# The look-up of expert numbers in a routed layer, split into a short and a long half

## The chip, the cores and the metric

The kernel runs on one core of a Trainium2 chip. The metric is the device time of one execution in microseconds (us). The core has a tensor engine (PE), a vector engine (DVE), a scalar engine (ACT), GpSimd (POOL) and a queue engine (SP), which run on their own and wait for one another by semaphores, and 16 DMA engines.

## The reference

One layer over 1024 tokens of 1024 fp32 numbers: a mixing sublayer (window attention beside a gated delta rule), and a sublayer that routes each token to single experts. The routing is what matters here:

```python
q = jnp.einsum('bsd,de->bse', h, w_query).reshape(B, S, PEER_HEADS, 2, PEER_QUERY_DIM // 2)
scores = jnp.einsum('bshpd,hpnd->bshpn', q, sub_keys)
s_top, i_top = lax.top_k(scores, K)                                   # K = 16, 8 heads, 2 x 128 keys
cand = (s_top[..., 0, :, None] + s_top[..., 1, None, :]).reshape(B, S, PEER_HEADS, K * K)
best, ci = lax.top_k(cand, K)
expert = i1 * N_KEYS + i2              # i1, i2: the keys of candidate ci
gates = jax.nn.softmax(best, axis=-1)
...
u = jnp.take(expert_u, et, axis=0)     # 128 experts for each token
act = jax.nn.gelu(jnp.einsum('tkd,td->tk', u, xt), approximate=False) * gt
return jnp.einsum('tk,tkd->td', act, jnp.take(expert_v, et, axis=0))
```

So each token reads 128 rows of `expert_u` and 128 of `expert_v`, of 4 KB each: 1.07 GB for the whole sequence.

## The kernel before, in words

The tokens are cut into 8 tiles of 128. A tile's work on the way to its experts is written as pieces numbered 0 to 49, and each engine has its own part of a piece. Pieces 0 to 22 are the mixing and the layer norm after it, 23 to 30 the products with the query weights (PE alone), 31 to 36 the search for the 16 best keys of each of the 16 key sets, and 37 to 49 the rest of the routing on DVE:

- Piece 37 forms the candidates. The 16 best of 256 sums can only be among 50 pairs (i, j), those with (i+1)(j+1) at most 16. `PAIR_ROWS` lists them by blocks, and for each block one addition writes the sums (`cand`) and one the expert numbers (`cid`), over all 8 heads: 14 additions at L2001.
- Pieces 38 and 39 find the 16 best candidates of each head in order, as values (`best`) and as places 0 to 49 (`fbest`).
- Pieces 40 to 47 look up the expert numbers, a head each. L2035 compares 16 ranks x 50 places, L2039 multiplies the hits with the numbers, and L2042 sums each rank's 50. Each of the three waits for the one before it.
- After piece 47 PE turns the numbers (piece 48, L1273). DVE copies them in pieces 48 (L2050) and 49 (L2066) into what POOL reads, and releases POOL by `g_tile`. POOL then gathers: 128 rows of U (one slot for 128 tokens, L944) and 128 of V (one token's 128 experts, L952, or L964 and L969 where V rows also go into U's buffers), each an indirect DMA of 512 KB.

DVE multiplies each U row with the tokens (the dot products, L2074), and PE sums V rows with the gates as weights (L1326). U and V have 8 buffers each. POOL waits at L943 until DVE or PE has freed a U buffer.

The order of pieces is written out by hand in tables of "halves": after each two dot products (or four in tile 0) every engine does the pieces that its table puts at this half. Tile 0 has nothing beside its pieces but input projections (units of 8 matmuls at L301, done by PE beside pieces 0 to 22 and 31 to 41, in its order ahead of piece 48). Tile 1's pieces go beside and after tile 0's dot products by `VECTOR_AT`: pieces 37 to 49 stand at halves 70 to 83, past the last dot product, mixed with pieces 1 to 4 of tile 2 (`EARLY_MIX`). Among those, piece 2 writes the coefficients that PE waits for at L1154, and piece 4 waits for PE at L1722. Tile 2's routing pieces stand at halves 33 to 61 of tile 1's dot products (`FIRST_TAIL`), between the mixing of tile 3. From then on a loop does the same for each tile (`TAIL` and `MIX`).

The lists of a tile (`top`, `itop`, `ftop`, `cand`, `cid` and so on) are views of one stretch of 2048 numbers in each partition, `arena` for tile 0 and the last eighth of `wq` for the others; `eq`, the 800 hits, lies over `top`, `itop` and `ftop`, which are read out by then. `gl` holds the gelu of the dot products, `actT` its transpose, from which ACT fills the columns of weights (`fill`).

Of the kernel before, what the change touches and what calls it, by code (L numbers as in the profile page):

```python
# [18 lines left out]
P = 128  # L19
# [8 lines left out]
PH, NK, TOPK = 8, 128, 16  # L28
SLOTS = PH * TOPK
# [6 lines left out]

PAIR_ROWS = [(0, 1, 16, 0), (1, 2, 8, 16), (2, 3, 5, 24), (3, 4, 4, 29), (4, 5, 3, 33), (5, 8, 2, 36), (8, 16, 1, 42)]
NCAND = 50
LEAST = -3.0e38
NU = 8  # L40
NV = 8
# [71 lines left out]
CONST_COLS = {}  # L113
_at = 0
for _name, _n in (("ident", P), ("upto", P), ("after", P), ("decay_mask", P), ("ones", 1), ("chunk_of", 2),
                  ("level", 6 * P), ("ident_a", P), ("dist", 192), ("dist_past", 64), ("iota50", 50)):
    CONST_COLS[_name] = (_at, _at + _n)
    _at += _n
NCONST = _at
# [16 lines left out]
def constant_table():  # L136

    t = np.zeros((P, NCONST), np.float32)

    def put(name, a):  # L140
        lo, hi = CONST_COLS[name]
        t[:, lo:hi] = a.reshape(a.shape[0], -1)
# [10 lines left out]
    for l in range(6):  # L153
        b = 1 << l
        j, i = r[:, None], r[None, :]
# [7 lines left out]
    dist = np.where(ok, np.abs(q - k), FAR).astype(np.float32)  # L163
    put("dist_past", dist[:, 0:64])
    dist[:, 0:64] = FAR
    put("dist", dist)
    put("iota50", np.tile(np.arange(50, dtype=np.float32)[None], (P, 1)))
    return t


def build(nc, consts, x, ln_in_g, ln_in_b, w_in, conv_w, a_sinks, b_a_log, b_dt_bias, b_norm_w, w_out,
          ln1_g, ln1_b, w_query, sub_keys, expert_u, expert_v, ln2_g, ln2_b, out):
    fp32, u32 = mybir.dt.float32, mybir.dt.uint32
    ALU, ACT, AX = mybir.AluOpType, mybir.ActivationFunctionType, mybir.AxisListType

    ctx = ExitStack()
    with ctx:
        def sb(name, shape, dt=fp32, c=ctx):
            return c.enter_context(nc.sbuf_tensor(name, shape, dt))
# [7 lines left out]
        s_dve = sem("s_dve")  # L187
# [5 lines left out]
        def const(name):  # L193
            lo, hi = CONST_COLS[name]
            return C[:, lo:hi]
# [477 lines left out]
        h1T = view(0, KD, P)  # L673
        qT = view(1024, 2 * PH, P)
        w_part = view(1024, 2 * PH * P)
        Lists = namedtuple("Lists", "top itop ftop cand cid best ibest fbest fex den eq")

        def lists(at):

            return Lists(at(0, 2 * PH, TOPK), at(256, 2 * PH, TOPK, dt=u32), at(512, PH, 2, TOPK),  # L680
                         at(800, PH, NCAND), at(1200, PH, NCAND), at(1600, PH, TOPK), at(1728, PH, TOPK, dt=u32),
                         at(1856, PH, TOPK), at(800, PH, TOPK), at(1984, 2, PH), at(0, TOPK, NCAND))

        def last_view(at, *dims, dt=fp32):
            return shaped(wq[:, KD - 1, at:at + int(np.prod(dims))], dims, dt)
# [3 lines left out]
        def lists_for(t):  # L689

            return lists_of[0 if isinstance(t, int) and t == 0 else 1]
# [27 lines left out]
        eidx = sb("eidx", [P, 2, SLOTS], u32, c=b)  # L719
        eidxT = sb("eidxT", [P, 2, P], u32, c=b)  # L720
        dots = sb("dots", [P, SLOTS], c=b)
        gl = sb("gl", [P, SLOTS], c=b)
        actT = sb("actT", [P, P], c=b)
        turned_query = V[:, 4, :].rearrange("p (b k n) -> p b k n", b=2, n=P)
        st2 = stb

# [150 lines left out]
        with nc.Block() as block:  # L877
# [802 lines left out]
            def _(dve):  # L1680
# [123 lines left out]

                def piece(n, t):
                    beta = gates[:, 1, t, :]
                    top, itop, ftop, cand, cid, best, ibest, fbest, fex, den, eq = lists_for(t)
                    if n == 0:
                        nc.vector.tensor_tensor(gU, per_head(const("upto")), bc3(gates[:, 0, t, :]), ALU.mult).then_inc(s_dve, 1)
                        nc.vector.tensor_tensor(bI, per_head(ident), bc3(beta), ALU.mult).then_inc(s_dve, 1)  # L1810
# [178 lines left out]
                    elif n == 37:  # L1989
# [5 lines left out]
                        dve.sem_inc(s_dve, -1)  # L1995

                        tv = top.rearrange("p (h q) k -> p h q k", q=2)
                        for dst, src in ((cand, tv), (cid, ftop)):
                            for i0, i1, w, at in PAIR_ROWS:
                                o = dst[:, :, at:at + (i1 - i0) * w].rearrange("p h (i j) -> p h i j", j=w)  # L2000
                                nc.vector.tensor_tensor(o, src[:, :, 0, i0:i1].unsqueeze(3).to_broadcast([P, PH, i1 - i0, w]),  # L2001
                                                        src[:, :, 1, 0:w].unsqueeze(2).to_broadcast([P, PH, i1 - i0, w]),
                                                        ALU.add).then_inc(s_dve, 1)
                        dve.wait_ge(s_dve, 2 * len(PAIR_ROWS))
                        dve.sem_inc(s_dve, -(2 * len(PAIR_ROWS)))
                    elif n == 38:
                        for h in range(PH):
                            nc.vector.max(best[:, h, 0:8], cand[:, h, :]).then_inc(s_dve, 1)
# [22 lines left out]
                        dve.sem_inc(b_soft, 1)  # L2031
                    elif 40 <= n <= 47:

                        for h in range(n - 40, n - 39):
                            nc.vector.tensor_tensor(eq, const("iota50").unsqueeze(1).to_broadcast([P, TOPK, NCAND]),  # L2035
                                                    fbest[:, h, :].unsqueeze(2).to_broadcast([P, TOPK, NCAND]), ALU.is_equal).then_inc(s_dve, 1)
                            dve.wait_ge(s_dve, 1)
                            dve.sem_inc(s_dve, -1)
                            nc.vector.tensor_tensor(eq, eq, cid[:, h, :].unsqueeze(1).to_broadcast([P, TOPK, NCAND]), ALU.mult).then_inc(s_dve, 1)  # L2039
                            dve.wait_ge(s_dve, 1)  # L2040
                            dve.sem_inc(s_dve, -1)
                            nc.vector.reduce_sum(fex[:, h, :], eq, AX.X).then_inc(s_dve, 1)  # L2042
                            dve.wait_ge(s_dve, 1)
                            dve.sem_inc(s_dve, -1)
                        if n == 47:
                            dve.sem_inc(b_fex, 1)
                    elif n == 48:
# [78 lines left out]
                def at(table, half, t):  # L2126
                    for n in pieces(table, half):
                        piece(n, t)
# [97 lines left out]
```

## Time and profile before

| what | value |
|---|---|
| runs | 3569.82, 3569.83, 3563.52 us (median 3569.82) |
| the profiled execution | 3557.49 us, of it the span 3555.7 us |
| busy in the span | PE 2133.0, DVE 2129.1, POOL 2186.9, ACT 380.0 us |
| moved by DMA | 1191.67 MB, of it 1073.87 MB by POOL's gathers |

The span is from the first to the last instruction. A line in the profile names an engine, a line of the kernel and the tiles it writes and reads; "idle before" is how long the engine stood still ahead of it, and the arrow says what ended that, where a "q" after the engine's name is a wait of its own instruction queue at that line.

### The profile page before, as it was taken

What the parts mean: (1) busy time and instruction counts of PE and PEld (TensorE: products, weight loads), DVE (VectorE), ACT (ScalarE), POOL (GpSimd) and SP (SyncE); (2) the same over time, 40 slices, a digit from 0 to 9 for tenths busy, and PEclk for the clock granted to TensorE, in tenths of its full rate; (3) what the DMA queues carried; (4) which work ended last, traced back from release to release, by engine and by line L of the source; (5) the groups of instructions that cost most, each with busy time, mean ns of one, the idle gap of its engine ahead of it and who ended that gap; (6) DMA issues with size and microseconds to landing.
All of it is one profiled execution on the core that took longest, in us unless ns stands there. A gap on an engine that the chain in (4) does not pass through costs nothing. (4 is left out here: it accounts for less than half of the span.)

```text
span 3555.7 us, 32715 instructions
## 1 busy us (share of the span) xinstructions
PE 2133.0 (60%) x9905; PEld 1065.0 (30%) x9905; DVE 2129.1 (60%) x4910; ACT 380.0 (11%) x697; POOL 2186.9 (62%) x2079
## 2 busy tenths in 40 slices
PE   6899967576756746564656466646574333333354
PEld 4665746324324323221412142214221000100011
DVE  3343277776676787567856785678567654544400
ACT  2231123111010010001100110011000000000000
POOL 1000025775653667777777777777777777777775
PEclk9999989777676777775877677857785555566578
DMA  8514247997975989999999999999999999999998
GB/s 274 164 57 119 61 147 256 362 346 294 370 279 198 340 318 373 406 406 395 371 407 405 389 366 408 403 391 376 406 409 403 386 383 400 387 409 409 392 402 338
DMA packets 400092, 1191.67 MB, mean 335 GB/s; under 512 B 54737, under 2 KB 122658, under 8 KB 397986
## 3 DMA queue, kind: packets, MB, share of 16 engines
q0 software_dynamic: 294912, 1073.87, 78.4%
q1 hardware_dynamic: 39970, 75.68, 5.9%
q10 hardware_dynamic: 65024, 39.89, 3.9%
q8 instruction: 86, 1.41, 0.2%
q14 instruction: 100, 0.82, 0.1%
HBM read 1168.29 MB, written 21.00 MB: 334 GB/s over the span
## 5 line engine op out<-in xcount | busy, mean ns | idle before, releaser
L2074 DVE CUSTOM_DVE_ANT_0 U<-U,h1c 128x1024 f32<-128x1024 f32 x940 | 1133.6, 1226 | 656.0 <-DMA U<-in_expert_u,eidx 602.8
L944 POOL DMA_INDIRECT U<-in_expert_u,eidx x1024 | 1100.4, 1075 | 490.3 <-issue 278.7
L1326 PE MATMUL bank<-V,ZH 128*32 128x512 f32 x3712 | 728.0, 926 | 1012.0 <-DMA V<-in_expert_v,eidxT 989.9
L952 POOL DMA_INDIRECT V<-in_expert_v,eidxT x832 | 881.4, 1059 | 286.2 <-issue 225.5
L1326 PEld LDWEIGHTS bank<-V,ZH 128*32 128x32 f32 x3712 | 145.6, 146 | 1486.8 <-issue 1486.7
L301 PE MATMUL bank<-V,U 128*128 128x387 f32 (+2 forms) x1056 | 316.3, 459 | 11.2 <-PEq L299 11.1
L974 POOL COPY eidx<-eidx_n 128x128 uint32<-128x128 uint32 x8 | 3.2, 402 | 443.0 <-POOLq L973 443.0
L301 PEld LDWEIGHTS bank<-V,U 128*128 128x128 f32 x1056 | 201.5, 193 | 116.3 <-issue 19.7
L1131 PE MATMUL bank<-wq,arena 128*128 128x512 f32 x400 | 188.7, 620 | 8.9 <-PEq L1254 8.9
L1084 PE MATMUL bank<-arena 128*128 128x512 f32 x224 | 118.9, 676 | 27.5 <-PEq L1090 14.0
L363 DVE SCALAR_TENSOR_TENSOR U<-bank,U 128x384 f32<-128x384 f32 (+3 forms) x108 | 61.8, 572 | 117.6 <-DVEq L358 107.0
L2074 DVE CUSTOM_DVE_ANT_0 U<-U,ZH 128x1024 f32<-128x1024 f32 x84 | 100.4, 1224 | 38.1 <-DMA U<-in_expert_u,eidx 32.5
L1555 ACT COPY ZH<-actT 128x16 f32<-128x16 f32 x64 | 13.3, 221 | 1016.5 <-ACTq L1554 1016.5
L1770 DVE BATCH_NORM_STATS2 stb<-pre 128x6 f32<-128x512 f32 x32 | 20.6, 684 | 167.5 <-DVEq L2084 166.3
L964 POOL DMA_INDIRECT V<-in_expert_v,eidxT x96 | 93.2, 971 | 38.8 <-issue 23.9
L969 POOL DMA_INDIRECT U<-in_expert_v,eidxT x96 | 93.2, 971 | 35.5 <-issue 25.4
L1131 PEld LDWEIGHTS bank<-wq,arena 128*128 128x128 f32 x400 | 76.8, 198 | 113.2 <-issue 113.2
L1326 PE MATMUL bank<-U,ZH 128*32 128x512 f32 x384 | 60.2, 756 | 47.0 <-DMA U<-in_expert_v,eidxT 47.0
L2074 DVE DVE_READ_ACCUMULATOR2_ANT dots<- 128x1 f32 x1024 | 84.3, 82 | 0.0
L1032 PE MATMUL bank<-raw 128*128 128x128 f32 x256 | 60.0, 322 | 35.4 <-PEq L1029 35.4
L1101 PEld LDWEIGHTS bank<-lnr,C 32*128 32x128 f32 x512 | 74.8, 230 | 20.0 <-issue 20.0
L1101 PE MATMUL bank<-lnr,C 32*128 32x128 f32 x512 | 79.0, 322 | 0.8 <-PEq L1349 0.8
(298 smaller groups left out, 2590.5 us busy)
## 6 DMA issues: line engine op xcount, KB each, us to landing
arena<-in_w_out SPq DMA_DIRECT2D x56, 512.0 KB, 6.9
U<-in_w_in ACTq DMA_DIRECT2D x36, 512.0 KB, 3.9
U<-in_expert_u,eidx POOLq DMA_INDIRECT x1024, 6.8
V<-in_expert_v,eidxT POOLq DMA_INDIRECT x928, 6.8
raw<-proj_dram SPq DMA_DIRECT2D x8, 1344.0 KB, 24.6
wq<-in_w_query SPq DMA_DIRECT2D x4, 2048.0 KB, 15.6
proj_dram<-U ACTq DMA_DIRECT2D x42, 192.0 KB, 1.9
arena<-w_dram SPq DMA_DIRECT2D x6, 1024.0 KB, 8.0
```

The lines of the kernel that those rows point to most:

```text
L301: last = nc.tensor.matmul(unit_ps[v % 2][:, 0:past + n], wbuf[:, load % 4, k, :], hT[:, k, lo - past:lo + n], start=k == 0, stop=k == KD - 1)
L363: nc.vector.scalar_tensor_tensor(y, ps, cw[:, i:i + 1], y, ALU.mult, ALU.add).then_inc(s_dve, 1)
L944: pool.indirect_dma_start(U[:, c % NU, :], None, expert_u[0], rows(ap=eidx[:, e, c:c + 1], axis=0)).then_inc(g_u[c % NU], 16)
L952: pool.indirect_dma_start(V[:, c % NV, :], None, expert_v[0], rows(ap=eidxT[:, e, token:token + 1], axis=0)).then_inc(g_v[c % NV // 2], 16)
L964: pool.indirect_dma_start(V[:, c % 16, :], None, expert_v[0], index).then_inc(g_v[c % 16 // 2], 16)
L969: pool.indirect_dma_start(U[:, c % 16 - 8, :], None, expert_v[0], index).then_inc(g_u[c % 16 - 8], 16)
L1032: nc.tensor.matmul(g[1][:, h * P:(h + 1) * P], XT[:, h, :], Pm[:, h, :], start=True, stop=True)
L1084: return nc.tensor.matmul(b0[:, 512 * n:512 * n + 512], yT[:, k, :], w[:, 512 * n:512 * n + 512], start=k == 0, stop=k == KD - 2)
L1101: last = nc.tensor.matmul(banks[1 + i][:, c * P:(c + 1) * P], ident[0:4 * KD, j:j + 1].to_broadcast([4 * KD, P]), lnr[:, :], start=True, s ...
L1131: last = nc.tensor.matmul(o, h1T[:, k, :], w[:, 512 * group:512 * group + 512], start=k == 0, stop=k == KD - 1)
L1326: last = nc.tensor.matmul(acc_ps[NSTEP * j:NSTEP * j + NSTEP, 512 * n:512 * n + 512], Zb[:, at - i:at - i + NSTEP], buf[j][:, 512 * n:512 ...
L2074: ins = nc.vector.tensor_tensor_reduce(out=U[:, c % NU, :], in0=U[:, c % NU, :], in1=rows, scale=1.0, scalar=0.0, op0=ALU.mult, op1=ALU.ad ...
```

## The change

The look-up is split by rank. Ranks 0 to 7 can only come from the 20 pairs with (i+1)(j+1) at most 8; for these, piece 37 forms a list of their own (`first`, by `FIRST_ROWS`, four more additions), and their places among the 50 are a constant row (`iota_first`, 20 columns more in the table of constants). Each of the three steps is now two instructions, one over 8 ranks x 20 places and one over 8 x 50, with one wait behind both. The lists are packed anew, and `gl` is no longer a tile of its own but the tile `actT`.

```diff
@@ -36,6 +36,8 @@
 PAIR_ROWS = [(0, 1, 16, 0), (1, 2, 8, 16), (2, 3, 5, 24), (3, 4, 4, 29), (4, 5, 3, 33), (5, 8, 2, 36), (8, 16, 1, 42)]
 NCAND = 50
+FIRST_ROWS = [(0, 1, 8, 0), (1, 2, 4, 8), (2, 4, 2, 12), (4, 8, 1, 16)]
+NFIRST = 20
@@ -113,7 +115,7 @@
-                  ("level", 6 * P), ("ident_a", P), ("dist", 192), ("dist_past", 64), ("iota50", 50)):
+                  ("level", 6 * P), ("ident_a", P), ("dist", 192), ("dist_past", 64), ("iota50", 50), ("iota_first", NFIRST)):
@@ -165,6 +167,9 @@
     put("iota50", np.tile(np.arange(50, dtype=np.float32)[None], (P, 1)))
+    starts = [at + (i - i0) * w for i0, i1, w, at in PAIR_ROWS for i in range(i0, i1)]
+    first = [starts[i] + j for i0, i1, w, at in FIRST_ROWS for i in range(i0, i1) for j in range(w)]
+    put("iota_first", np.tile(np.array(first, np.float32)[None], (P, 1)))
@@ -673,13 +678,14 @@
         def lists(at):
 
-            return Lists(at(0, 2 * PH, TOPK), at(256, 2 * PH, TOPK, dt=u32), at(512, PH, 2, TOPK),
-                         at(800, PH, NCAND), at(1200, PH, NCAND), at(1600, PH, TOPK), at(1728, PH, TOPK, dt=u32),
-                         at(1856, PH, TOPK), at(800, PH, TOPK), at(1984, 2, PH), at(0, TOPK, NCAND))
+            return Lists(at(0, 2 * PH, TOPK), at(256, 2 * PH, TOPK, dt=u32), at(560, PH, 2, TOPK),
+                         at(816, PH, NCAND), at(1216, PH, NCAND), at(1616, PH, TOPK), at(1744, PH, TOPK, dt=u32),
+                         at(1872, PH, TOPK), at(816, PH, TOPK), at(2000, 2, PH), at(0, 8, NCAND),
+                         at(400, PH, NFIRST), at(944, 8, NFIRST))
@@ -719,8 +725,8 @@
-        gl = sb("gl", [P, SLOTS], c=b)
         actT = sb("actT", [P, P], c=b)
+        gl = actT
@@ -1995,14 +2001,14 @@
-                        for dst, src in ((cand, tv), (cid, ftop)):
-                            for i0, i1, w, at in PAIR_ROWS:
+                        for dst, src, table in ((cand, tv, PAIR_ROWS), (cid, ftop, PAIR_ROWS), (first, ftop, FIRST_ROWS)):
+                            for i0, i1, w, at in table:
...
-                        dve.wait_ge(s_dve, 2 * len(PAIR_ROWS))
-                        dve.sem_inc(s_dve, -(2 * len(PAIR_ROWS)))
+                        dve.wait_ge(s_dve, 2 * len(PAIR_ROWS) + len(FIRST_ROWS))
+                        dve.sem_inc(s_dve, -(2 * len(PAIR_ROWS) + len(FIRST_ROWS)))
@@ -2031,17 +2037,23 @@
-                        for h in range(n - 40, n - 39):
-                            nc.vector.tensor_tensor(eq, const("iota50").unsqueeze(1).to_broadcast([P, TOPK, NCAND]),
-                                                    fbest[:, h, :].unsqueeze(2).to_broadcast([P, TOPK, NCAND]), ALU.is_equal).then_inc(s_dve, 1)
-                            dve.wait_ge(s_dve, 1)
-                            dve.sem_inc(s_dve, -1)
-                            nc.vector.tensor_tensor(eq, eq, cid[:, h, :].unsqueeze(1).to_broadcast([P, TOPK, NCAND]), ALU.mult).then_inc(s_dve, 1)
-                            dve.wait_ge(s_dve, 1)
-                            dve.sem_inc(s_dve, -1)
-                            nc.vector.reduce_sum(fex[:, h, :], eq, AX.X).then_inc(s_dve, 1)
-                            dve.wait_ge(s_dve, 1)
-                            dve.sem_inc(s_dve, -1)
+                        h = n - 40
+                        halves = ((0, NFIRST, const("iota_first"), eq_first, first), (8, NCAND, const("iota50"), eq, cid))
+                        for rank, width, places, hits, ids in halves:
+                            nc.vector.tensor_tensor(hits, places.unsqueeze(1).to_broadcast([P, 8, width]),
+                                                    fbest[:, h, rank:rank + 8].unsqueeze(2).to_broadcast([P, 8, width]),
+                                                    ALU.is_equal).then_inc(s_dve, 1)
+                        dve.wait_ge(s_dve, 2)
+                        dve.sem_inc(s_dve, -2)
+                        for rank, width, places, hits, ids in halves:
+                            nc.vector.tensor_tensor(hits, hits, ids[:, h, :].unsqueeze(1).to_broadcast([P, 8, width]),
+                                                    ALU.mult).then_inc(s_dve, 1)
+                        dve.wait_ge(s_dve, 2)
+                        dve.sem_inc(s_dve, -2)
+                        for rank, width, places, hits, ids in halves:
+                            nc.vector.reduce_sum(fex[:, h, rank:rank + 8], hits, AX.X).then_inc(s_dve, 1)
+                        dve.wait_ge(s_dve, 2)
+                        dve.sem_inc(s_dve, -2)
```

## Rows read from the trace of the kernel before

**Rows 1.** The page: busy times; DMA's busy tenths in 40 slices.
```profile
...
PE 2133.0 (60%) x9905; PEld 1065.0 (30%) x9905; DVE 2129.1 (60%) x4910; ACT 380.0 (11%) x697; POOL 2186.9 (62%) x2079
...
DMA  8514247997975989999999999999999999999998
...
```

**Rows 2.** Windows: stretch, us, busy times, PE clock, DMA share, GB/s.
```profile
...
800.00:900.00 100.00, 72.09 (x411) 46.63 (x404) 63.95 (x111) 11.06 (x23) 60.15 (x57) 0.78 0.80 299
...
1400.00:1500.00 100.00, 59.73 (x268) 24.69 (x264) 60.36 (x95) 4.62 (x8) 75.72 (x72) 0.76 1.02 404
...
1600.00:1700.00 100.00, 54.25 (x270) 23.75 (x270) 77.29 (x239) 18.11 (x32) 77.40 (x73) 0.64 1.01 391
...
3200.00:3500.00 300.00, 127.37 (x677) 30.37 (x677) 85.54 (x141) 7.71 (x17) 223.55 (x234) 0.70 1.01 402
...
```

**Rows 3.** Waits of 1300 to 3500 us, all engines and POOL alone.
```profile
...
DVE U L2074 <- DMA U<-in_expert_u,eidx: 590.3, 209, 8.1
...
POOL U L944 <- POOLq L943: 23.9, 52, 1.9
...
```

**Rows 4.** DVE's groups, shapes apart: busy us, mean ns, idle before.
```profile
...
L2035 DVE TENSOR_TENSOR wq<-C,wq 128x800 f32<-128x800 f32 x56 | 55.3, 987 | 1.5 <-DVEq L2030 0.2 <-DVEq L1853 0.2 <-DVEq L1731 0.2
...
L2001 DVE TENSOR_TENSOR wq<-wq 128x64 f32<-128x64 f32 x28 | 6.1, 218 | 0.4
...
```

**Rows 5.** Timeline of DVE, tile 0: start us, us, instruction, [idle before].
```profile
...
449.57 1.89 DVE L2001 TENSOR_TENSOR arena<-arena 128x128 f32<-128x128 f32 x14
...
484.02 0.99 DVE L2035 TENSOR_TENSOR arena<-C,arena 128x800 f32<-128x800 f32 x1
485.16 0.99 DVE L2039 TENSOR_TENSOR arena<-arena 128x800 f32<-128x800 f32 x1
486.30 0.98 DVE L2042 TENSOR_REDUCE arena<-arena 128x16 f32<-128x800 f32 x1
...
491.04 0.29 DVE L2066 CAST eidxT_n<-bank 128x128 uint32<-128x128 f32 x1 [2.19 <-DVEq L2065]
...
```

**Rows 6.** Timeline of PE, tile 0.
```profile
...
433.86 56.93 PE L301 MATMUL bank<-V,U 128*128 128x384 f32 x176
490.62 0.27 PE L1273 MATMUL bank<-C,arena 128*128 128x128 f32 x1
...
```

**Rows 7.** Timeline of DVE, tile 1.
```profile
...
778.55 1.22 DVE L1818 TENSOR_REDUCE sml<-arena 128x8 f32<-128x1024 f32 x1 [1.76 <-DVEq L1817]
...
823.51 0.43 DVE L1723 TENSOR_TENSOR arena<-bank,att 128x256 f32<-128x256 f32 x1 [4.01 <-DVEq L1722]
...
834.95 0.99 DVE L2042 TENSOR_REDUCE wq<-wq 128x16 f32<-128x800 f32 x1
...
```

**Rows 8.** Timeline of PE, tile 1.
```profile
...
808.72 1.94 PE L1156 MATMUL bank<-C,arena 128*128 128x128 f32 x8 [5.82 <-PEq L1154]
...
836.24 0.45 PE L1273 MATMUL bank<-C,wq 128*128 128x128 f32 x1 [7.86 <-PEq L1272]
...
```

**Rows 9.** Timeline of POOL, tile 1.
```profile
...
848.03 0.96 POOL L944 DMA_INDIRECT U<-in_expert_u,eidx  x1 [8.91 <-POOLq L943]
...
```

**Rows 10.** Timeline of DVE, tile 2.
```profile
...
1033.59 1.22 DVE L1818 TENSOR_REDUCE sml<-arena 128x8 f32<-128x1024 f32 x1 [0.26 <-DVEq L1817]
...
1164.41 0.99 DVE L2035 TENSOR_TENSOR wq<-C,wq 128x800 f32<-128x800 f32 x1
...
1205.96 1.22 DVE L2074 CUSTOM_DVE_ANT_0 U<-U,h1c 128x1024 f32<-128x1024 f32 x1
...
1214.87 1.22 DVE L2074 CUSTOM_DVE_ANT_0 U<-U,h1c 128x1024 f32<-128x1024 f32 x1 [0.23 <-DMA U<-in_expert_u,eidx]
...
```

**Rows 11.** Timeline of POOL, tile 2.
```profile
...
1172.39 0.94 POOL L944 DMA_INDIRECT U<-in_expert_u,eidx  x1 [3.67 <-POOLq L943]
...
```

**Rows 12.** Timelines of PE and DVE: output projection's last slice, its reader.
```profile
...
1192.23 3.75 PE L1084 MATMUL bank<-arena 128*128 128x512 f32 x4 [3.66 <-PEq L1237]
...
1198.13 1.22 DVE L1940 SCALAR_TENSOR_TENSOR pre<-pre,bank 128x1024 f32<-128x1024 f32 x1
...
```

More of the change, by code:

```diff
@@ L675, in build @@
         w_part = view(1024, 2 * PH * P)
-        Lists = namedtuple("Lists", "top itop ftop cand cid best ibest fbest fex den eq")
+        Lists = namedtuple("Lists", "top itop ftop cand cid best ibest fbest fex den eq first eq_first")
         def lists(at):
-            return Lists(at(0, 2 * PH, TOPK), at(256, 2 * PH, TOPK, dt=u32), at(512, PH, 2, TOPK),
-                         at(800, PH, NCAND), at(1200, PH, NCAND), at(1600, PH, TOPK), at(1728, PH, TOPK, dt=u32),
-                         at(1856, PH, TOPK), at(800, PH, TOPK), at(1984, 2, PH), at(0, TOPK, NCAND))
+            return Lists(at(0, 2 * PH, TOPK), at(256, 2 * PH, TOPK, dt=u32), at(560, PH, 2, TOPK),
+                         at(816, PH, NCAND), at(1216, PH, NCAND), at(1616, PH, TOPK), at(1744, PH, TOPK, dt=u32),
+                         at(1872, PH, TOPK), at(816, PH, TOPK), at(2000, 2, PH), at(0, 8, NCAND),
+                         at(400, PH, NFIRST), at(944, 8, NFIRST))
         def last_view(at, *dims, dt=fp32):
@@ L1806, in piece @@
                     beta = gates[:, 1, t, :]
-                    top, itop, ftop, cand, cid, best, ibest, fbest, fex, den, eq = lists_for(t)
+                    top, itop, ftop, cand, cid, best, ibest, fbest, fex, den, eq, first, eq_first = lists_for(t)
                     if n == 0:
```

## The prediction

> **What bounds the kernel now.** I read the profile from the whole to the part. The page comes first: vector engine (DVE), tensor engine (PE) and GpSimd (POOL) are each busy for about 60% of the span, and the DMA digits are 9 from slice 16 on [rows 1]. No engine's share says anything yet, so the windows come next. From about 1300 us to the end the DMA engines are full (share 1.01 to 1.02), at 391 to 404 GB/s; in the window at 800 us they are not (0.80) [rows 2]. The waits of the stretch 1300 to 3500 say the same from the other side: the dot products wait 590 us for gathered rows, and POOL waits only 24 us for DVE to free a buffer [rows 3]. So in tiles 3 to 7 DVE work is hidden under the gathers: what it saves there only lengthens a wait for DMA. Their look-ups lie there.
>
> That leaves the look-ups of tiles 0, 1 and 2. For each I looked in the timelines for what ends the wait behind them.
>
> **What one look-up costs, before and after.** Before, a head takes three dependent instructions over 16 x 50 = 800 elements: 0.99 us each, begun 1.14 us apart, so the wait between them costs 0.15 us [rows 5]. A head is 3 x 1.14 = 3.41 us.
> After, each of the three steps is two instructions that don't depend on each other, over 8 x 20 = 160 and 8 x 50 = 400 elements, and then one wait. Their durations: 64 elements take 218 ns and 800 take 987 ns [rows 4], a slope of 769/736 = 1.045 ns an element and a fixed part of 151 ns. That gives 318 and 569 ns. The trace of before shows what two such instructions cost in a row: the 14 of L2001 (800 elements together) run without a wait in 1.89 us [rows 5], while their durations sum to 0.84 + 14 x 0.151 = 2.95 us; each of 13 joints hides (2.95 - 1.89)/13 = 82 ns. So a step is 318 - 82 + 569 = 805 ns, with the wait 0.955 us, and a head 2.87 us: **0.55 us less a head, 4.4 us a tile**.
> The reduction is costed as the others, since with 800 elements it shows the same 0.99 us [rows 5].
>
> Added: four additions in piece 37 for the short list, 160 elements in all: 0.167 + 4 x (0.151 - 0.082) = **0.44 us a tile**. Net 4.0 us of DVE time a tile, 32 us in all.
>
> The bounds of the unshown: if the joints hid nothing, a head would be 3 x (0.318 + 0.569 + 0.15) = 3.11 us, a saving of 0.30 a head; if the short instruction cost only its elements, 3 x (0.167 + 0.569 + 0.15) = 2.66, a saving of 0.75. I take 0.55, which is the row nearest in kind.
>
> The 20 more constant columns are 10 KB in one load of many. That gl now lies in actT adds no wait: the gelu writes it after the last fill has read it, on the same engine, and the copy back into it already waited for the transpose that reads gl. It costs nothing; if that order were otherwise, one ScalarE wait a tile would show before the gelu. The repacked lists overlay only lists that are read out: the short list goes over itop after its copy to ftop, the short hits over cand after the last search.
>
> **Tile 0: nothing.** Here the look-up stands straight before the first gather, and one would book all 4 us. But PE runs eleven projection units back to back from 433.86 to 490.79 us and turns the expert numbers only then, at 490.62 [rows 6], while DVE is done with the last head at 487.28 and waits 2.19 us for that transpose [rows 5]. The saving lengthens this wait to 6 us. DVE would have to lose over 3 us here before it cost anything.
>
> **Tile 1: 2.8 us.** DVE has no dot products then; its order is piece 37, heads 40 to 42, the coefficients of tile 2's mixing, heads 43 to 45, piece 4 of that mixing, heads 46 and 47. The 0.44 us of piece 37 vanish in a wait of 1.76 us behind it [rows 7]. The three first heads save 1.67 us, and PE, which waited 5.82 us for the coefficients [rows 8], starts that much earlier. The next three heads save nothing: DVE already waits 4.01 us for PE behind them [rows 7], and what they save lengthens it. The last two pass whole: 1.11 us. PE waits 7.86 us for the last head, at 836.24 [rows 8]; behind this wait stand tile 0's last weighted sums, and they free the buffers for which POOL waits until 848.03 before it gathers for tile 1 [rows 9]. Its own wait on the indices is over by then. So 1.67 + 1.11 = 2.8 us, and the restart of the gathers moves by it.
>
> **Tile 2: 2.5 us.** Its pieces stand between the dot products of tile 1, 1030 to 1217 us. Behind piece 37 the wait is only 0.26 us [rows 10], so 0.44 us is paid. Up to 1172 us POOL again and again waits for DVE to free a buffer, last for 3.67 us [rows 11]. Heads 40 to 44 lie before that, and the waits for PE between them follow DVE's own results, so they pass: 5 x 0.55 = 2.8 us. From there on the gathers run as fast as the DMA takes them, and the dot products find their rows just in time: the first wait on DMA is at 1214.87 [rows 10]; at one U row per 1.9 us (three gathers of 0.524 MB for two U rows, at 404 GB/s), the row read at 1205.96 us, five dot products before, had landed about 0.7 us earlier. Heads 45 to 47 (1.7 us) can thus gain at most about 0.7. I take 0.2: 2.8 - 0.44 + 0.2 = 2.5. The other thing that could hold DVE, the last slice of the output projection, ends at 1195.98, 2.1 us before DVE reads it at 1198.13 [rows 12], room enough.
>
> **Sum:** 2.8 + 2.5 = 5.3 us. From about 1290 us the DMA is full to the end and every later event moves by this. Against the profiled execution: 3557.49 - 5.3 = 3552.2 us. The median of the runs is 3569.82, 12.3 us above that execution, though one of the three is 3563.52; the same step off the median gives **3564.5 us**, 0.15% faster. About 0.2%, 7.1 us, is what a measurement of this kernel can tell from no change, so I forecast a small gain that counts as the same.
>
> **The rivals.**
> *Instructions don't overlap.* If every instruction costs its 0.151 us and the 0.15 us of a wait as well, six are 6 x 0.301 + 3 x 560 x 1.045 ns = 3.56 us a head against 3.41, and the four additions 1.37 us. Tile 1 then loses 5 x 0.15 = 0.8, tile 2 1.37 + 1.2 = 2.6: +3.4 us, 3573.2. The 14 additions in 1.89 us speak against it: by this price they would take 5.1 us [rows 5]. The Trainium skill's page "VectorE: DVE Perf Modes", section "The DRAIN you can't avoid", says this: a next instruction starts only when the pipeline is empty, and leaving out semaphores between them saves nothing, so that only the count of instructions matters. By that rule the doubled count is a loss; the trace does not agree, with 14 in 1.89 us. Chance 0.04.
> *The DMA swallows it.* If the gathers between 848 and 1290 us are nearer to their limit than the shares say (the 800 window has 0.80 [rows 2]), the saving there only turns into waits: 0 to -3 us, 3568.5. For it: DMA is at 1.0 in parts of it; against: POOL's waits of several us [rows 9, 11]. Chance 0.20. That the change saves DVE next to nothing belongs here too.
> *More passes.* If tile 0's 4.0 us passed as well (PE's last units being set by something that DVE releases), or the 0.75 of the upper bound held with heads 45 to 47 whole, the gain is 8 to 9.5 us: 3561, faster by 0.25%. Rows 6 speak against the first. Chance 0.22.
> *The gathers slow down (the slower side).* All tiles behind the constants start some 80 to 96 bytes further on (their rows grow by 80 bytes), U and V too, into which 1.07 GB is gathered. The gathers fill 2250 us; from a loss of 0.55% (12.4 us) on it outweighs the gain by over 0.2%. Rates in full windows are 404, 402 and 391 GB/s [rows 2], so 1%, a third of their spread, is my price: +22.5 - 5.3 = +17 us, 3587. No row shows an address at work. The Trainium skill's "DMA: Bandwidth & Descriptors", section "How a descriptor splits into AXI transactions", says that a transfer that doesn't start on 256 bytes costs beats more; no run here shows it. Chance 0.06.
>
> **How the numbers follow.** The forecast (-3 to -7 us) has 0.48, the others 0.20, 0.22, 0.06 and 0.04. Faster by over 0.2% takes the rival with more passing and some of the forecast's near edge: 0.27. Slower takes the gathers: 0.07. The rest, 0.66, is the same. The range reaches down past the rival where more passes, by the 5 us between runs, to 3555, and up past the rival without overlap to 3574; only the slow gathers and the tails are left out.
>
> **What would show it.** Groups of 160 and 400 elements at about 0.32 and 0.57 us, the second begun 0.24 us after the first; a head begun every 2.9 us in tile 0; before the copy of the turned indices in tile 0 a wait of 6 us and not 2.2, with the first gather where it was, 495.6 us; PE's transpose in tile 1 2.8 us earlier and the restart of the gathers at about 845.2; the wait of 4.01 us grown to 5.7; the last slice of tile 2's output projection in time and the first wait of a dot product on DMA some microseconds before 1214.87; the same rate of gathers behind 1300 us, and longer waits for U rows. I am wrong if pairs don't overlap, if the first gather moves, or if the rate behind 1300 us changes: half a percent there outweighs all the rest.

## The result: 3539.39 us, 0.8% faster, and the profile after

The changed kernel takes 3539.39 us (median of 4 runs, 3535.14 to 3542.43), the kernel before 3569.14 beside it: ratio 0.9919, interval 0.9902 to 0.9936. I had forecast 3564.5 with a range down to 3555. On three other chips the same kernel gave 0.9947, 0.9948 and 0.9959 (below), so by the ratios the gain is 15 to 19 us there and 29 us here; the runs don't show why the first pair differs. Profiled execution against profiled execution it is 3535.14 against 3557.49 us, 22.4 us.

The page of the kernel after, busy times and DMA digits, answers to [rows 1]:

```profile
...
PE 2129.5 (60%) x9905; PEld 1062.0 (30%) x9905; DVE 2098.6 (59%) x5134; ACT 379.8 (11%) x697; POOL 2160.2 (61%) x2079
...
DMA  8524247998976989999999999999999999999998
...
```

DVE is busy for 30.5 us less (32 forecast). POOL is busy for 26.7 us less, which no step of the prediction has: it issues the same 2048 gathers.

The windows, as [rows 2]:

```profile
...
800.00:900.00 100.00, 70.63 (x409) 44.64 (x409) 64.57 (x133) 11.06 (x23) 63.08 (x60) 0.85 0.84 314
1400.00:1500.00 100.00, 57.97 (x254) 24.37 (x254) 55.00 (x99) 3.21 (x8) 72.69 (x70) 0.72 1.03 406
1600.00:1700.00 100.00, 56.49 (x298) 26.22 (x290) 78.32 (x221) 16.74 (x31) 77.97 (x72) 0.72 1.00 380
3200.00:3500.00 300.00, 135.19 (x725) 31.94 (x725) 73.83 (x121) 7.70 (x17) 222.76 (x233) 0.71 1.01 400
...
```

By these the stretch from 1400 us on looks as before, and the last one not even faster. The shares could not show where the time went. The gathers can: every one is a row of POOL, the same 2048 in the same order, so I compared when gather number k starts (from 0, times from each profile's own rows), after minus before: number 0 -2.3 us (1.8 of it were there when tile 0's first look-up instruction began, at 458.33 for 460.15 us), 256 -5.0, 384 -14.9, 1472 -14.5, 1552 -23.9, the last -22.1. So the time came from two places: gathers 256 to 383 (beside tile 2's look-up) and gathers 1472 to 1551 (beside tile 7's). Between them, from gather 384 to 1472, beside the look-ups of tiles 3 to 6, nothing was gained (1542.6 and 1543.0 us). Windows of just these two stretches, before:

```profile
...
942.82:1227.15 284.33, 178.47 (x708) 101.30 (x708) 202.76 (x509) 26.56 (x50) 140.84 (x130) 0.69 0.79 281
2769.72:2883.54 113.82, 36.49 (x164) 6.82 (x160) 74.18 (x109) 0.67 (x3) 89.45 (x81) 0.54 0.99 377
...
```

and after:

```profile
...
937.79:1212.27 274.48, 172.99 (x707) 97.55 (x708) 198.94 (x537) 26.55 (x50) 140.52 (x129) 0.73 0.80 286
2755.23:2859.66 104.43, 36.41 (x160) 6.80 (x160) 69.20 (x129) 0.67 (x3) 80.02 (x80) 0.50 1.02 405
...
```

The first is 9.9 us shorter. In the second, 113.8 has become 104.4 us, and POOL's busy time for its 80 gathers fell by as much, from 89.45 to 80.02 us: the gathers themselves got shorter.

### The profile page after: what moved, and what is told of

Same layout as the page of the kernel before. It is cut to its first block and busy times, and to the rows that moved or that the text cites. A ratio compares the mean times of both kernels' runs of the same rounds, so it can differ in the third digit from the quotient of the medians.

```text
span 3533.3 us, 32939 instructions
## 1 busy us (share of the span) xinstructions
PE 2129.5 (60%) x9905; PEld 1062.0 (30%) x9905; DVE 2098.6 (59%) x5134; ACT 379.8 (11%) x697; POOL 2160.2 (61%) x2079
## 5 line engine op out<-in xcount | busy, mean ns | idle before, releaser
L958 POOL DMA_INDIRECT V<-in_expert_v,eidxT x832 | 863.3, 1038 | 296.4 <-issue 228.4
L368 DVE SCALAR_TENSOR_TENSOR U<-bank,U 128x384 f32<-128x384 f32 (+3 forms) x108 | 61.8, 572 | 117.3 <-DVEq L363 106.7
L970 POOL DMA_INDIRECT V<-in_expert_v,eidxT x96 | 91.7, 955 | 38.9 <-issue 26.5
L1090 PEld LDWEIGHTS bank<-arena 128*128 128x128 f32 x224 | 47.6, 226 | 105.5 <-issue 104.1
```

The source lines that it names most:

```text
L368: nc.vector.scalar_tensor_tensor(y, ps, cw[:, i:i + 1], y, ALU.mult, ALU.add).then_inc(s_dve, 1)
L958: pool.indirect_dma_start(V[:, c % NV, :], None, expert_v[0], rows(ap=eidxT[:, e, token:token + 1], axis=0)).then_inc(g_v[c % NV // 2], 16)
L970: pool.indirect_dma_start(V[:, c % 16, :], None, expert_v[0], index).then_inc(g_v[c % 16 // 2], 16)
L1090: return nc.tensor.matmul(b0[:, 512 * n:512 * n + 512], yT[:, k, :], w[:, 512 * n:512 * n + 512], start=k == 0, stop=k == KD - 2)
```

## What the steps of the prediction show after

Durations. DVE's groups, shapes apart (busy us, mean ns), as [rows 4]:

```profile
...
L2049 DVE TENSOR_TENSOR wq<-wq 128x400 f32<-128x400 f32 x56 | 32.9, 587 | 0.0
...
L2043 DVE TENSOR_TENSOR wq<-C,wq 128x160 f32<-128x160 f32 x56 | 18.2, 326 | 1.8 <-DVEq L1737 0.6 <-DVEq L1859 0.2 <-DVEq L2036 0.2
...
L2054 DVE TENSOR_REDUCE wq<-wq 128x8 f32<-128x160 f32 x56 | 17.9, 320 | 8.2
...
```

Forecast 318 and 569 ns, measured 320 to 326 and 559 to 587. Tile 0 on DVE's timeline, as [rows 5]: two heads' first comparisons, and the copy of the turned numbers:

```profile
...
458.33 0.81 DVE L2043 TENSOR_TENSOR arena<-C,arena 128x160 f32<-128x160 f32 x2 [0.24 <-DVEq L2036]
...
461.18 0.81 DVE L2043 TENSOR_TENSOR arena<-C,arena 128x160 f32<-128x160 f32 x2
...
488.79 0.29 DVE L2078 CAST eidxT_n<-bank 128x128 uint32<-128x128 f32 x1 [5.83 <-DVEq L2077]
...
```

A pair takes 0.81 us and a head 2.85 (forecast 0.805 and 2.87), and the wait behind tile 0's last head is 5.83 us (forecast 6). Tile 0 gave nothing, as forecast.

Tile 1, as [rows 7 to 9]: DVE behind the three heads, PE's two waits, and POOL's restart:

```profile
...
820.32 0.42 DVE L1729 TENSOR_TENSOR arena<-bank,att 128x256 f32<-128x256 f32 x1 [5.93 <-DVEq L1728]
...
```

```profile
...
805.21 1.94 PE L1162 MATMUL bank<-C,arena 128*128 128x128 f32 x8 [5.66 <-PEq L1160]
...
832.29 0.45 PE L1279 MATMUL bank<-C,wq 128*128 128x128 f32 x1 [6.86 <-PEq L1278]
...
```

```profile
...
843.17 0.96 POOL L950 DMA_INDIRECT U<-in_expert_u,eidx  x1 [7.99 <-POOLq L949]
...
```

The wait of 4.01 us grew to 5.93 (forecast 5.7), and the restart moved by 4.9 us, of which 2.3 were there at gather 0: 2.6 for a forecast of 2.8.

Tile 2 is where the early part went wrong. DVE's timeline before, two places at which it waits for PE between the heads:

```profile
...
1117.53 0.69 DVE L1745 TENSOR_TENSOR raw<-raw,bank 128x512 f32<-128x512 f32 x1 [4.44 <-DVEq L1744]
...
1160.02 0.69 DVE L1760 TENSOR_TENSOR St<-St,sml 128x512 f32<-128x512 f32 x1 [4.53 <-DVEq L1901]
...
```

and after, the same two and the reader of the last slice of the output projection [rows 12]:

```profile
...
1110.16 0.69 DVE L1751 TENSOR_TENSOR raw<-raw,bank 128x512 f32<-128x512 f32 x1 [1.79 <-DVEq L1750]
...
1148.48 0.69 DVE L1766 TENSOR_TENSOR St<-St,sml 128x512 f32<-128x512 f32 x1 [2.08 <-DVEq L1907]
...
1184.16 1.21 DVE L1946 SCALAR_TENSOR_TENSOR pre<-pre,bank 128x1024 f32<-128x1024 f32 x1
...
```

The waits fell from 4.44 and 4.53 us to 1.79 and 2.08, and the reader of the last slice begins 14.0 us earlier. PE's granted clock over the stretch is 0.73 against 0.69 before (windows above).

## The experiments

All ratios are to the kernel before on the same chip. "80 gathers" is the time from gather 1472 to 1552. The other two columns are medians over the eight heads of tile 7: "away" is the time from the first look-up instruction of a head to the next dot product, "ahead" the time by which that dot product begins before the next gather.

| kernel | ratio (interval) | gathers 256 to 384, us | away, us | ahead, us | 80 gathers, us |
|---|---|---|---|---|---|
| before | 1 | 284.3 | 3.44 | 1.04 | 113.8 |
| after (the first pair) | 0.9919 (0.9902 to 0.9936) | 274.5 | 2.94 | 0.75 | 104.4 |
| layout_only | 1.0001 (0.9988 to 1.0013) | 280.7 | 3.44 | 1.04 | 113.3 |
| lookup_only | 0.9946 (0.9926 to 0.9965) | 272.5 | 2.93 | 0.75 | 105.2 |
| early_tiles | 0.9998 (0.9985 to 1.0011) | 272.2 | 3.44 | 1.04 | 114.1 |
| late_tiles | 0.9975 (0.9963 to 0.9987) | 281.2 | 2.92 | 0.75 | 107.4 |
| after_again | 0.9947 (0.9926 to 0.9968) | 273.6 | 2.95 | 0.75 | 104.9 |
| with_filler | 1.0010 (1.0000 to 1.0021) | 277.7 | 3.43 | 0.25 | 114.1 |
| two_halves_of_50 | 1.0005 (0.9994 to 1.0016) | 284.0 | 3.66 | 0.02 | 109.9 |
| own_waits | 0.9981 (0.9970 to 0.9992) | 271.0 | 2.42 | 0.22 | 114.1 |
| added_two_inputs | 0.9963 (0.9945 to 0.9981) | 276.9 | 4.5 | 0.42 | 111.2 |
| added_one_input | 0.9955 (0.9939 to 0.9971) | 274.4 | 4.41 | 0.51 | 111.4 |
| rank_by_rank | 1.0001 (0.9989 to 1.0013) | 281.0 | 3.13 | 0.54 | 111.6 |
| no_late_lookup | 0.9925 (0.9909 to 0.9941) | 273.9 | 0.35 | 0.83 | 102.8 |
| after_fourth | 0.9948 (0.9933 to 0.9964) | 272.4 | 2.93 | 0.75 | 105.4 |
| one_sum_late_again | 0.9989 (0.9976 to 1.0002) | 275.2 | 3.4 | 0.28 | 112.0 |
| own_waits_early_again | 0.9937 (0.9923 to 0.9951) | 271.3 | 2.92 | 0.74 | 106.7 |

**First: memory places or look-up, early or late tiles.** Both look-ups can stand in one kernel; a test on the tile number chooses:

```diff
+        def split(t):
+            return isinstance(t, int) and t <= 2      # early_tiles; late_tiles: its opposite; layout_only: False
```

lookup_only instead leaves U, V and all others where they were: the row of 20 places becomes a tile of its own, allocated last.

> All data where the changed kernel has it (20 more constant columns, gl in actT, lists packed anew, so U and V start 96 bytes further on), but the look-up of before, three instructions over 800 elements a head. Theory A, the saved vector time alone makes the gain: the time of before, within 3 us. Theory B, the places in memory make the gathers faster: 8 to 30 us faster than before, seen as more GB/s behind 1300 us.

> The new look-up, but U, V and all tiles ahead of them where they were in the kernel before: the row of 20 places is a tile of its own behind all others, with one more small load. Theory A: as the changed kernel, 22 to 30 us faster than before. Theory B: only what passes of the vector time, 5 us (my forecast) to 14 us (what the two traces show up to 1230 us).

> Changed kernel, but tiles 3 to 7 look up as before. Theory A with a gain only where the DMA isn't full: the whole gain of the two traces up to 1300 us, 14 to 15 us, and with my forecast's sizes alone 5 us. Theory C, that the look-ups of the later tiles matter too: 8 to 15 us less gain than the changed kernel's 30.

> Changed kernel, but tiles 0 to 2 look up as before. Theory A: nothing, within 2 us of before, since the DMA is full there. Theory C, that shorter two-input vector instructions let GpSimd write or read its descriptors sooner, or something else in the full stretch: 8 to 15 us faster. Theory B, the places in memory: 8 to 30 us faster, the same as the kernel with the places alone.

The places do nothing (1.0001), so the rival of slower gathers falls, and with it any credit to the layout. late_tiles gains 0.25% in tiles of which I had said that nothing can be gained. early_tiles has the whole early gain (272 us for gathers 256 to 384), yet ends at 0.9998, which no theory had. The two parts don't add up either: 0.02% and 0.25%, where both together give 0.53%.

**Second: is it DVE's time, or the long instruction?** with_filler has two more comparisons a head, two_halves_of_50 both halves over 50 places, own_waits no shared wait:

```diff
+                        nc.vector.tensor_tensor(spare, ...iota50, 8 x 32..., ALU.is_equal)           # with_filler, and 8 x 16 behind the products
-                        halves = ((0, NFIRST, const("iota_first"), eq_first, first), ...)
+                        halves = ((0, NCAND, const("iota50"), eq_low, cid), ...)                      # two_halves_of_50
-                        dve.wait_ge(s_dve, 2)
+                            dve.wait_ge(s_dve, 1 + n_done)                                            # own_waits: each half for its own half
```

> The changed kernel itself, as the measure for the three beside it: 0.991 to 0.994 of the kernel before, by every theory.

> The changed kernel with two more comparisons a head (256 and 128 elements, written to a spare place), so that DVE again takes about 3.4 us a head, but with no instruction over 0.6 us. Theory A (what counts is how long DVE is away from the dot products): the gain is gone, ratio 0.999 to 1.002. Theory C (what hurts is the long instruction of 800 elements while it runs): the gain stays, 0.991 to 0.995. If half comes back, both have a share.

> The changed kernel with both halves over all 50 places (400 and 400 elements), as many elements as before and twice the instructions, no list of 20. By the prices measured, a head is 3 x (2 x 0.57 - 0.08 + 0.15) = 3.6 us, 0.2 us more than before. Theory A: 1.000 to 1.003. Theory C: 0.992 to 0.996, although DVE is busy for longer.

> The changed kernel in which each half waits for its own half before it, so that the long instruction covers the wait of the short one: about 0.1 us less at each of the two inner joints, 0.2 to 0.3 us less a head. Theory A: as the change saves 0.55 us a head for 0.8%, this gives 0.3 to 0.45% more than the changed kernel, 0.987 to 0.990 of before. Theory C: as the changed kernel, within 0.1%.

The first two fit theory A (DVE's time counts) and not C, the third breaks both: own_waits takes 0.46 us less a head (2.39 against 2.85) than the changed kernel and loses to it, 0.9981 to 0.9947. Its windows, of gathers 256 to 384 and of the 80:

```profile
...
937.67:1208.67 271.00, 171.80 (x709) 97.16 (x708) 198.09 (x537) 26.44 (x50) 141.22 (x130) 0.70 0.79 286
2762.07:2876.12 114.05, 35.90 (x160) 6.84 (x160) 65.63 (x126) 0.67 (x3) 89.66 (x80) 0.59 0.97 365
...
```

The early stretch is the shortest of all (271.0 us), the late one back at 114. So what counts late isn't DVE's time.

**What lengthens a gather.** Beside tile 7's look-up nothing else is moved, and POOL hardly waits for a buffer. A gather lasts 0.94 us, with 0.30 us of issue behind it: 1.24 us. Many last longer. Before, POOL's timeline:

```profile
...
2835.52 1.75 POOL L952 DMA_INDIRECT V<-in_expert_v,eidxT  x1 [0.30 <-issue]
2837.58 0.94 POOL L944 DMA_INDIRECT U<-in_expert_u,eidx  x1 [0.30 <-issue]
...
```

and DVE's at the same time:

```profile
...
2834.34 0.98 DVE L2035 TENSOR_TENSOR wq<-C,wq 128x800 f32<-128x800 f32 x1
2835.47 0.99 DVE L2039 TENSOR_TENSOR wq<-wq 128x800 f32<-128x800 f32 x1
2836.60 0.99 DVE L2042 TENSOR_REDUCE wq<-wq 128x16 f32<-128x800 f32 x1
...
```

The gather of 2835.52 begins while the product (two SBUF inputs, until 2836.46) runs, and lasts 1.75 us. The one of 2837.58, at the last moment of a sum, lasts 0.94. In all rows I read one rule holds: **a gather that begins while DVE runs an instruction with two SBUF inputs lasts 0.94 us plus what is left of that instruction 0.13 us after the gather's start**; here 2836.46 - 2835.65 = 0.81, and 0.94 + 0.81 = 1.75. An instruction that began less than about 0.04 us before the gather, or after it, doesn't count, and neither does one that reads one of its inputs from PSUM (the tile `bank`): 816 of 829 gathers begun inside such a one lasted 0.94 us. Of the 256 gathers from number 1472 on, in each of 20 traces of the kernels above and below, the rule gives every one within 0.05 us with at most one exception, in rank_by_rank with eight; 43 to 69 of the 256 were lengthened by more than 0.05 us, the worst by 1.05. Over all 2048 gathers it misses 11 to 21 a trace (80 in rank_by_rank). And the 80 gathers take 80 x 1.241 = 99.3 us plus the sum of the lengthenings: 14.2 us before (of it 7.8 by dot products), 4.8 after, 14.5 in own_waits (12.9 by dot products). That gives 113.5, 104.1 and 113.8, against 113.8, 104.4 and 114.1 measured.

This is a rule of the Trainium skill, page "SBUF — State Buffer", section "Who interferes with whom": a DVE instruction with two SBUF inputs contends with a GpSimd instruction that reads SBUF, the shared port is locked exclusively, and on this chip a `tensor_reduce` never contends. The trace agrees, by the rows above for the wait (0.81 us) and those below for the sum (0.94 us, no wait). The same section says that a probe did not find a `tensor_tensor` to hold up DMA, and infers that descriptors need only the write side; here the product did hold up the gather. I had not weighed any of it in the prediction.

After, POOL's timeline shows why the look-up cost nothing there:

```profile
...
2817.43 0.94 POOL L950 DMA_INDIRECT U<-in_expert_u,eidx  x1 [0.30 <-issue]
2818.68 0.94 POOL L950 DMA_INDIRECT U<-in_expert_u,eidx  x1 [0.31 <-POOLq L949]
2819.92 1.28 POOL L950 DMA_INDIRECT U<-in_expert_u,eidx  x1 [0.30 <-issue]
...
```

DVE's:

```profile
...
2816.24 0.81 DVE L2043 TENSOR_TENSOR wq<-C,wq 128x160 f32<-128x160 f32 x2
2817.20 0.84 DVE L2049 TENSOR_TENSOR wq<-wq 128x160 f32<-128x160 f32 x2
2818.18 0.80 DVE L2054 TENSOR_REDUCE wq<-wq 128x8 f32<-128x160 f32 x2
2819.17 1.23 DVE L2086 CUSTOM_DVE_ANT_0 U<-U,h1c 128x1024 f32<-128x1024 f32 x1 [0.19 <-DVEq L2056]
...
```

One gather begins 0.23 us into the pair of products, as the short one ends and the long one has barely begun, and one 0.50 us into the sums, at 0.94 us each; only the dot product of 2819.17 catches one, with 0.34 us left (1.28). The pattern of 2 dot products, a head, and 4 gathers repeats, so one good or bad meeting repeats too.

**Third: DVE's time against this rule.** added_two_inputs and added_one_input give DVE four more instructions a head in tiles 3 to 7; rank_by_rank has 16 short ones a head; no_late_lookup leaves the look-up of tiles 3 to 7 out, so it gathers other rows, as many as before.

```diff
+                                nc.vector.tensor_tensor(spare, ..., ALU.is_equal)               # two inputs: 256 and 112 elements, twice
+                                nc.vector.reduce_sum(spare[:, 0, 0:8], eq[:, :, 0:32], AX.X)    # or one input, the same sizes
+                                nc.vector.scalar_tensor_tensor(hits[:, r, :], places, fbest[:, h, rank + r:rank + r + 1], ids[:, h, :],
+                                                               ALU.is_equal, ALU.mult, accum_out=fex[...])   # rank_by_rank
+                            nc.vector.tensor_copy(fex[:, h, :], cid[:, h, 0:TOPK])               # no_late_lookup
```

> The changed kernel, and in tiles 3 to 7 behind each head four comparisons more, which read two SBUF tiles (256 and 112 elements, twice), about 1.4 us of DVE a head, 56 us in all; results go to a spare place. Theory P (a gather of POOL that starts while a DVE instruction with two SBUF inputs runs lasts 0.94 us plus what is left of that instruction, and POOL's own row of gathers sets the pace from tile 3 on): some gathers that start inside the added instructions last up to 0.3 us longer; the end is later than in its twin with one input, 0.999 to 1.004 against before. Theory A (only the time that DVE is away from the dot products counts): both twins are slower than the changed kernel by the same amount, at least 1%. Theory D (DMA is the bound, the change was worth only tile 2's part): both as the changed kernel, 0.993 to 0.996.

> The twin: the four added instructions are sums over the same 256 and 112 elements, so they read one tile and last about as long. Theory P: no gather that starts inside them is longer than 0.94 us on their account; the only change is the phase in which gathers meet the dot products. So less late than the twin with two inputs by 2 to 10 us, 0.993 to 1.000 against before. Theory A: as the twin. Theory D: 0.993 to 0.996.

> The changed kernel with one instruction for each rank (compare, multiply and sum over 20 or 50 places at once), so sixteen short ones a head that don't depend on each other and no wait but the last. From the slope and joint of short instructions, 8 x 0.09 + 8 x 0.12 + 0.15 = 1.8 us a head if reading the sum back is hidden, up to 4 us if each waits for it. Theory P: no gather can meet more than 0.2 us of such an instruction, so its look-ups add next to nothing to the gathers: with 1.8 us a head 0.985 to 0.991, with 4 us 0.995 to 1.000 (tile 2 loses). Theory A: 0.98 to 0.985 with 1.8 us, above 1.0 with 4 us. Theory D: 0.990 to 0.994 with 1.8 us.

> The changed kernel with the look-up of tiles 3 to 7 left out: each head's 16 numbers are a copy of its first 16 candidates, so other rows are gathered, as many as before. Says what the look-ups of these tiles still cost. Theory P: the stall of gathers by the look-ups' own instructions (by the trace of the changed kernel about 5 us in these tiles) goes, and the rest is the phase against the dot products, which may give or take 10 us: 0.985 to 0.996. Theory A: 0.980 to 0.985, since 23 us of DVE a tile go, five times what the change saved. Theory D: 0.993 to 0.996.

Theory A falls: 1.5 us more a head (12 us a tile) leave 0.9963 and 0.9955 where the changed kernel has 0.9947 (on another chip), and about 20 us less a tile give 0.9925, so either moves it by some 0.1 to 0.2%, within the intervals. The window of the 80 gathers without a look-up has 49.5 us of DVE in place of 69.2, and is only 1.6 us shorter than the changed kernel's:

```profile
...
2756.85:2859.66 102.81, 36.36 (x160) 6.79 (x160) 49.52 (x88) 0.67 (x3) 78.41 (x80) 0.67 1.02 408
...
```

The twins don't part as I expected (0.9963 and 0.9955, intervals overlap; 111.2 and 111.4 us, and theory P had 0.999 to 1.004 for the first): in both nearly all of the lengthening is by dot products, none by the added instructions. rank_by_rank, at 3.1 us a head between the two lengths foreseen, ends at 1.0001: its own instructions lengthen hardly a gather, its dot products do so by 12.0 us. What the changed work did was to shift the dot products. So a last theory: the length of a head decides at which **phase** the dot products behind it meet the gathers. The column "away" fits nothing monotonic: 0.35 gives 102.8 us, 2.42 114, about 2.9 104 to 107, 3.13 112, 3.43 114, 3.66 110, 4.4 to 4.5 111.

The column "ahead" is the phase itself, and it sorts them. A gather that meets this dot product waits for 1.23 - 0.13 = 1.10 us, less the time "ahead". With 0.75 or 0.83 us ahead the 80 gathers take 103 to 107 us, with 0.42 to 0.54 111 to 112, with 0.22 to 0.28 112 to 114; at 0.02 (two_halves_of_50) the dot product begins too late to hold that gather, and they take 110. The kernels with the old look-up stand apart: 1.04 us ahead costs that gather next to nothing, but they lose 6.4 us to the products of 800 elements and 7.8 to dot products. with_filler has a head of the same length, loses nothing to products and 14.5 us to dot products. That both come to 114 us is chance, and the length of a head alone doesn't set the phase.

**Fourth: phase alone, and both gains in one kernel.** one_sum_more_late puts a sum over 400 elements, one input, into the last group of each head of tiles 3 to 7; nothing uses its result (DVE waits for its end with the two other sums). own_waits_early has own_waits in tiles 0 to 2 and the shared waits from tile 3 on.

```diff
+                        if late:
+                            nc.vector.reduce_sum(spare, eq, AX.X).then_inc(s_dve, 1)
```

Their first runs fell on a chip on which all kernels take about 3750 us: windows late in the kernel show 361 to 367 GB/s there, and from gather 384 on POOL stands waiting for 200 to 234 us, where it waits 68 to 88 on the other chips, so transfers and buffers, not POOL, set the late pace. Ratios there: the changed kernel 0.9959 (0.9936 to 0.9982), with the sum 0.9970 (0.9946 to 0.9993), own_waits_early 0.9939 (0.9917 to 0.9960); the 80 gathers take 114 us in all three (104 to 107 had been expected for the first and the last), though their lengthenings are 6.0, 14.6 and 7.5 us. On a chip like the first:

> One sum more a head in tiles 3 to 7, one input, head as long as before the change. Theory F (phase by the head's length): gathers 1472 to 1551 take 112 to 115 us, and the ratio is 0.994 to 0.998. Theory G (the long two-input instructions themselves): 104 to 105 us and 0.991 to 0.995. The last chip already showed 14.6 us of lengthened gathers there against 6.0 of the changed kernel, but its transfers hid the difference.

> Heads of 2.39 us in tiles 0 to 2, of 2.87 us from tile 3 on. On the last chip 0.9939 beside 0.9959 of the changed kernel. If early and late gain add up: gather 384 17 to 19 us earlier than before the change, gathers 1472 to 1551 in 104 to 107 us, ratio 0.989 to 0.993 and below the changed kernel's by about 0.001.

POOL's timeline with the sum:

```profile
...
2805.59 0.94 POOL L950 DMA_INDIRECT U<-in_expert_u,eidx  x1 [0.31 <-POOLq L949]
2806.83 1.94 POOL L950 DMA_INDIRECT U<-in_expert_u,eidx  x1 [0.30 <-issue]
...
```

DVE's:

```profile
...
2805.10 0.97 DVE L2054 TENSOR_REDUCE wq<-wq 128x8 f32<-128x160 f32 x2
2805.99 0.56 DVE L2057 TENSOR_REDUCE wq<-wq 128x8 f32<-128x400 f32 x1
2806.73 1.23 DVE L2089 CUSTOM_DVE_ANT_0 U<-U,h1c 128x1024 f32<-128x1024 f32 x1 [0.19 <-DVEq L2059]
...
```

The gather of 2805.59 begins inside a sum, and lasts 0.94. The dot product here begins 0.10 us before a gather instead of 0.75, and that gather waits for nearly all of it: 1.94 us. This is the worst of the eight heads; in six of them it begins 0.28 us before. The window of the 80:

```profile
...
2772.53:2884.53 112.00, 36.41 (x160) 6.83 (x160) 71.60 (x135) 0.67 (x3) 87.63 (x80) 0.58 0.99 374
...
```

It has 112.0 us against 105.4 of the changed kernel beside it (lengthenings 12.4 against 5.8 us, nearly all by dot products), and the ratio is 0.9989 against 0.9948, above the 0.994 to 0.998 that theory F had. An instruction with one input, whose result nothing uses, took most of the gain back, and beside tile 7 all of the loss is in gathers that met a dot product: there the phase is shown. own_waits_early keeps the early gain (gather 384 starts 20.5 us earlier than in the profile of before, the changed kernel's 15.4) and the good phase (106.7 us). With 0.9937 beside 0.9948, and 0.9939 beside 0.9959 on the other chip, it has the lowest ratio of the versions with the whole look-up on each of these two chips, though just above the 0.989 to 0.993 expected, and each pair of intervals overlaps.

## Why the prediction was wrong, by its steps

- **"So in tiles 3 to 7 DVE work is hidden under the gathers" and "every later event moves by this": the step that failed.** Measured: 9.4 of the 22.4 us came beside tile 7's look-up. I read a DMA share of 1.01 to 1.02 [rows 2] as a bound of the transfers. But the trace also held POOL's own bound: its gathers of 0.94 us and 0.30 us of issue are 1.24 us each, 423 GB/s at 0.524 MB, so at 404 GB/s POOL had almost no room. Beside tile 7, where POOL waits for no buffer, any lengthening of a gather was lost. From gather 384 to 1472 it was not so: the changed kernel's gathers were lengthened by 6.5 us less, but POOL waited 6.9 us more, and no time was gained. DVE's time was hidden indeed (no_late_lookup, the twins); where its instructions stand against the gathers was not.
- **Tile 2, "2.5 us": mis-sized.** For gathers 256 to 384 the changed look-up needs 272.2 to 274.5 us (the changed kernel, lookup_only, early_tiles, after_again, after_fourth; mean 273.1), the old one 280.7 to 284.3 (before, layout_only, late_tiles; mean 282.1): 9.0 us, and 8.1 if the four other kernels with the same look-up in tiles 0 to 2 are taken in (added_two_inputs, added_one_input, no_late_lookup, one_sum_late_again; mean of the nine 274.0). DVE's busy time in it gives 3.8 (202.76 to 198.94), all eight heads less the additions and not five heads. The rest is less waiting, mostly for PE. Which wait shrinks differs from run to run (in layout_only one of the two shown is short too). PE's granted clock in this stretch goes along with a part of it: 0.694 to 0.709 in the three old ones, 0.710 to 0.737 in the nine new ones. The pairs nearest in clock, 0.708 and 0.709 (280.7 and 281.2 us) against 0.710 and 0.713 (276.9 and 273.9), differ by 5.5 us. Whether the change or chance gave the higher clock was not tested: this part stays open.
- **Tile 1, "2.8 us"**: right in mechanism and size (2.6; over the profiles with the new look-up and the old ones the difference scatters by 3 us). **Tile 0, nothing**: right, with the wait that grew to 5.8 us.
- **Prices of the instructions**: right within 4%, the 82 ns hidden at a joint too (the row of 176 matmuls is 22 units of 8, not eleven; nothing rests on it). The rival in which instructions don't overlap, and behind it the rule of the Trainium skill's page "VectorE: DVE Perf Modes", section "The DRAIN you can't avoid", had no part in it: a pair takes 0.81 us where its durations sum to 0.89.
- **The range**: "half a percent there outweighs all the rest" was written of slower gathers alone. That they could get faster had no rival and no chance.
- **Where early_tiles loses its early gain.** Its profile is 14.3 us ahead at gather 384, 11 at 1408, 5 at 1472 and level at the end. In every trace the time from gather 384 to the last is 2063.8 us, plus the lengthenings, plus POOL's other waits: 167.0 and 70.3 us before, 183.5 and 68.0 in early_tiles. So all of the loss is longer gathers. layout_only, with the look-up of before in all tiles, has 176.4 and 74.6, so single profiles differ by 9 us in this alone. That old heads meet the gathers at other phases there would fit, and wasn't tried.

## What to carry to other kernels

When POOL's gathers set the pace, compare one gather with its issue (here 1.24 us) to the pitch of the gathers before calling DMA the bound, and read what makes single gathers longer. A gather begun inside a DVE instruction with two SBUF inputs waited for its end, so a small change in DVE's order can move the total by phase and not by work (here 0.9948 to 0.9989 by one sum more a head): measure such a change, and don't credit the work that it saves.

## What the runs showed of the hardware

- The wait of a gather for DVE is sharp: 0.94 us plus the rest of the two-input instruction, to 0.05 us, over 5120 gathers with 9 exceptions. A cast with one input (128x256, uint32 to fp32) did the same, by 0.11 us for five gathers of the trace before, so two inputs are not the only case.
- DVE is held in turn, but briefly: a dot product that began within about 0.04 us of a gather's start lasted up to 1.31 us, the others 1.22 to 1.23 beside gathers (680 of the 705 longer ones in the 20 traces began so).
- Sixteen fused instructions of 20 or 50 elements begin 0.16 and 0.20 us apart (240 to 270 ns each, with a read of the sum between them), so one head by ranks takes 3.1 us, no less than three pairs (2.9).
- One chip moved 362 GB/s in its window of 3200 to 3500 us (after_third) where the first moved 400 to 402, and took about 3750 us.
